# Attention products with the values: one burst for eight units, with sixteen buffers of turned probabilities

## The reference

```python
# group A: 8 heads of 64, each query sees a clamped 8 x 16 window of a 32 x 64 grid, plus a learned bias
logits = einsum('bnmqhd,bnmkhd->bnmhqk', qb, kb) * scale + bias     # masked
p = softmax(logits);  o = einsum('bnmhqk,bnmkhd->bnmqhd', p, vb)
# group B: 8 query heads on 2 key heads, |q - k| <= 128, with a sink logit per head
m = maximum(max(logits), sink)
p = exp(logits - m);  denom = sum(p) + exp(sink - m)
o = einsum('bnkgqj,bnjkd->bnqkgd', p / denom, vb)
```

## Time and profile before

| | |
|---|---|
| median of 3 runs | 2333.44 us (2331.61 to 2334.02) |
| the profiled execution | 2332.78 us, its span 2331.0 us |
| PE busy | 2223.8 us, 95% of the span |
| DVE, ACT, POOL busy | 1445.7, 922.2, 331.8 us |
| values products L890 | 1632 matmuls, 118.9 us busy, inside the attention phase |
| mean granted TensorE clock | 0.984 |

### The profile page before, as it was taken

The page is one execution under the profiler, slowest core; times in us unless marked ns, Lnnn a source line. Parts: engine busy times, 40 slices in busy tenths (PEclk is TensorE's granted clock), DMA queues, the critical chain, the costliest instruction groups (busy, mean ns, idle before and its releaser), DMA issues.

```text
span 2331.0 us, 33582 instructions
## 1 busy us (share of the span) xinstructions
PE 2223.8 (95%) x11592; PEld 1832.8 (79%) x11592; DVE 1445.7 (62%) x2761; ACT 922.2 (40%) x1790; POOL 331.8 (14%) x308
## 2 busy tenths in 40 slices
PE   7999999699979989979999999999999999999998
PEld 5888888677857868857888888788888878788886
DVE  5411023289898857768666666856565667666676
ACT  4311122178858833325333333533333333232333
POOL 6301300244390000001111212000000001010100
PEclk9999999899999999989999999999999999999999
DMA  8534333599952145666454546532323276353544
GB/s 244 160 136 136 94 98 103 147 246 245 233 149 82 55 147 202 213 233 222 172 185 167 187 165 228 200 127 77 135 78 127 69 289 234 118 173 111 176 150 153
DMA packets 278071, 376.78 MB, mean 162 GB/s; under 512 B 15578, under 2 KB 184546, under 8 KB 273328
## 3 DMA queue, kind: packets, MB, share of 16 engines
q1 hardware_dynamic: 269920, 354.21, 47.7%
q0 software_dynamic: 5568, 11.87, 2.1%
q10 hardware_dynamic: 2448, 8.91, 1.3%
HBM read 237.84 MB, written 140.31 MB: 162 GB/s over the span
## 4 chain that ended last, share of the span: by engine, by line
PE 51%; DVE 2%; DMA 1%; issue 0%; ACT 0%; DVEq 0%; ACTq 0%
PE ff_psum L1842 12%; PE ff_psum L1843 12%; PE ff_psum L1844 12%; PE ff_psum L1876 6%; PE ff_psum L1878 5%; PE ff_psum L1877 5%; DVE ff_a L1671 1%; DMA ff_raw<-in_w_gate 0%; DVE ff_x L1769 0%; DVE ff_d L1665 0%; DMA ff_d<-down_scratch 0%; DVE ff_ring L1652 0%; DVE ff_h L1657 0%; DVE ff_x L1782 0%; ACT ff_d L1541 0%
## 5 line engine op out<-in xcount | busy, mean ns | idle before, releaser
L1842 PE MATMUL ff_psum<-ff_h,ff_ring 128*128 128x512 f32 x1232 | 480.9, 390 | 14.8 <-DVE ff_ring L1652 12.5
L1843 PE MATMUL ff_psum<-ff_h,ff_ring 128*128 128x512 f32 x1232 | 480.5, 390 | 0.0
L1844 PE MATMUL ff_psum<-ff_h,ff_ring 128*128 128x512 f32 x1232 | 480.3, 390 | 0.0
L1842 PEld LDWEIGHTS ff_psum<-ff_h,ff_ring 128*128 128x128 f32 x1232 | 231.9, 188 | 63.9 <-DVEq L1718 12.9
L1843 PEld LDWEIGHTS ff_psum<-ff_h,ff_ring 128*128 128x128 f32 x1232 | 232.1, 188 | 48.2
L1844 PEld LDWEIGHTS ff_psum<-ff_h,ff_ring 128*128 128x128 f32 x1232 | 231.9, 188 | 48.3
L1876 PE MATMUL ff_psum<-ff_d,ff_a 128*128 128x512 f32 x616 | 240.6, 391 | 8.2 <-DVE ff_x L1769 5.4
L1877 PE MATMUL ff_psum<-ff_d,ff_a 128*128 128x512 f32 x616 | 239.8, 389 | 0.0
L1878 PE MATMUL ff_psum<-ff_d,ff_a 128*128 128x512 f32 x616 | 239.7, 389 | 0.0
L1769 DVE TENSOR_TENSOR ff_x<-ff_psum,ff_x 128x512 f32<-128x512 f32 x224 | 153.8, 690 | 123.3 <-PE ff_psum L1878 123.0
L1652 DVE TENSOR_TENSOR ff_ring<-ff_raw,ff_ring 128x512 fp32r<-128x512 f32 x176 | 129.7, 739 | 106.0 <-ACT ff_ring L1532 106.0
(11 more groups left out here) (149 smaller groups left out, 4136.6 us busy)
## 6 DMA issues: line engine op xcount, KB each, us to landing
acts_scratch<-ff_acts SPq DMA_DIRECT2D x22, 1792.0 KB, 7.4
ff_a<-acts_scratch SPq DMA_DIRECT2D x24, 960.0 KB, 5.0
ff_raw<-in_w_gate SPq DMA_DIRECT2D x42, 512.0 KB, 3.8
ff_raw<-in_w_up SPq DMA_DIRECT2D x42, 512.0 KB, 4.0
att_q_stack<-qk_scratch SPq DMA_DIRECT2D x64, 256.0 KB, 5.2
ff_d<-down_scratch SPq DMA_DIRECT2D x21, 768.0 KB, 6.5
ffn_in_scratch<-mix_h_stage SPq DMA_DIRECT2D x8, 1792.0 KB, 6.2
ff_h<-ffn_in_scratch SPq DMA_DIRECT2D x14, 1024.0 KB, 8.4
```

What stands on the lines that cost most here:

```text
L1842: pe.matmul(out_bank, whi[:, k], hhi[:, :, k], start=(k == 0 and not onto), stop=False, skip_group_check=onto)
L1843: pe.matmul(out_bank, whi[:, k], hlo[:, :, k], start=False, stop=False, skip_group_check=onto)
L1844: last = pe.matmul(out_bank, wlo[:, k], hhi[:, :, k], start=False, stop=(k == 3), skip_group_check=onto)
```

## The change

`values` does nothing in seven of eight units; in the last of a block (u % 8 = 7) it waits once and then issues the products of all four tiles, 24 or 32 (22 where a tile has two chunks) times a chunk's pair of heads. The buffers of turned probabilities grow from 4 to 16. `pv_done` counts blocks instead of tiles, and the waits on it are rewritten to match. Lags, order of stages and every other buffer stay.

```diff
-    SC_BUFS, SN_BUFS, PT_BANKS, PT_BUFS, O_BANKS = 4, 8, 2, 4, 2
+    SC_BUFS, SN_BUFS, PT_BANKS, PT_BUFS, O_BANKS = 4, 8, 2, 16, 2
+    GROUP = 8
@@ advance (SyncE)
-                        sp.wait_ge(pv_done, PT_BUFS // 2 + NT * r + 4 * (b + 1))
+                        sp.wait_ge(pv_done, 2 + 4 * r + b + 1)
@@ copy_turned (ACT)
-                act.wait_ge(pv_done, PT_BUFS // 2 + NT * r + u // 2 - 1)
+                act.wait_ge(pv_done, 4 * r + u // GROUP + 1)
@@ results (DVE)
-                dve.wait_ge(pv_done, PT_BUFS // 2 + NT * r + 4 * (b + 1))
+                dve.wait_ge(pv_done, 2 + 4 * r + b + 1)
@@ values (PE)
-                if u % 2 == 0:
+                if u % GROUP != GROUP - 1:
                     return
-                t = u // 2
-                b, n = t // 4, kind.chunks(t)
-                for i in kind.new_portions(t):
-                    pe.wait_ge(v_in[i], 16 * (r + 1) if kind.near else 16 * (NEAR_ROUNDS + 1))
+                b = u // GROUP
+                for t in range(4 * b, 4 * b + 4):
+                    for i in kind.new_portions(t):
+                        pe.wait_ge(v_in[i], 16 * (r + 1) if kind.near else 16 * (NEAR_ROUNDS + 1))
                 pe.wait_ge(pt_copied, PT_BANKS + UNITS * r + u + 1)
-                if t % 4 == 0:
-                    pe.wait_ge(o_copied, 4 * r + b + 1)
-                for j in range(n):
-                    v = v_sb[:, kind.value_chunk(t, j), :]
-                    for e in range(2):
-                        h = slice(e * HD, (e + 1) * HD)
-                        last = pe.matmul(op[h, b % 2, t % 4 * P:(t % 4 + 1) * P], v[:, h],
-                                         pt[:, (u - 1 + e) % PT_BUFS, j * P:(j + 1) * P],
-                                         start=(j == 0), stop=(j == n - 1))
+                pe.wait_ge(o_copied, 4 * r + b + 1)
+                for t in range(4 * b, 4 * b + 4):
+                    n = kind.chunks(t)
+                    for j in range(n):
+                        v = v_sb[:, kind.value_chunk(t, j), :]
+                        for e in range(2):
+                            h = slice(e * HD, (e + 1) * HD)
+                            last = pe.matmul(op[h, b % 2, t % 4 * P:(t % 4 + 1) * P], v[:, h],
+                                             pt[:, (2 * t + e) % PT_BUFS, j * P:(j + 1) * P],
+                                             start=(j == 0), stop=(j == n - 1))
                 last.then_inc(pv_done, 1)
-            pe.sem_inc(pv_done, PT_BUFS // 2)
+            pe.sem_inc(pv_done, 2)
```

## The result

The changed kernel takes 2361.11 us (median of 4, 2355.85 to 2363.20), the kernel before 2333.73 (median of 4): a ratio of 1.0115, 95% interval 1.0096 to 1.0133, so it is slower by 27 us. The forecast was 2354, and slower. The profiled execution took 2355.85 us, with a span of 2354.0: against the profiled one of before, 2332.78, that is 23.1 us where the sum gave 21.5.

What follows compares the result with a forecast made beforehand. The prediction took PE to bound the attention phase, with DVE and ACT close behind. Loops lengthened by uncovered bursts summed to 21.5 us more, added to the profiled 2332.8: 2354 us, range 2340 to 2364.

Steps and rivals of the forecast that it cites:

- 0.34 us for each visit to the products: PE's passage between tile forms around a visit to the products; 96 fewer visits take 33 us off PE's time.
- The burst is not covered: Attention phase: ACT stands still during PE's burst; its copies and exps make a 10.3 us loop against 9.5 on average before.
- Window rounds 41.1: Sum of four block loops in a window round, 10.1, 10.3, 10.8 and 9.9 us: 3.2 us more than before.
- Near rounds 45.2: Sum of four block loops in a near round, 11.6, 11.9, 11.0 and 10.7 us: 1.8 us more than before.
- 1.5 for GpSimd: Near rounds: GpSimd's bias making slows DVE's normalise, now on the loop's path; 1.5 us a round, between 0 and some 5.
- The other terms: Remaining shares of the sum by round, such as 1 us for round 0 and 2.5 each for rounds 3 and 4.
- PE's idle time: Expected sign: in window rounds it rises from 3% to some 20%, ahead of the turn and released by ACT's copy.
- DMAs don't move: SyncE's waits on `pv_done` stay for a block's last tile, some 2 us later; next round's values are needed a round later.
- the third rival: Nothing measurable: loss in window rounds and gain in near ones cancel, within 5 us of 2333; chance 0.06.
- PE as the bound: Rival: PE stays the bound in the attention phase, so the 33 us of passages come out, 2300 us; chance 0.06.
- DVE as the bound: Rival: the burst is hidden and DVE's own work bounds the rounds, 2320 us if half is met; chance 0.12.

Runs made afterwards that it cites:

- one_form: Kernel before with one full-width product per chunk instead of two half-width ones, head 1's share left out: 2313.67 us, 0.9919 of the kernel before.
- first_chunk: Changed kernel with only the first chunk's product of each tile, in the same bursts: 2320.75 us, 0.9940 of the kernel before.
- late_results: Changed kernel with DVE copying a block's results out in step u + 12 instead of u + 8: 2349.85 us, 1.0073 of the kernel before.
- few_bias: Changed kernel with GpSimd making one of six bias operations of each kind in near rounds 1 to 3: 2355.48 us, 1.0090 of the kernel before.
- group4: Changed kernel with the products of two tiles in one burst instead of four: 2331.59 us, 0.9985 of the kernel before.
- group4_late: Changed kernel with bursts of two tiles and the results' copy in step u + 12: 2343.32 us, 1.0042 of the kernel before.

## Why the prediction was right

- *PE bound the attention phase, with 0.34 us for each visit to the products.* Right but for one block in four of a window round: one_form shows the size (0.32 to 0.33) and the cause, and its cycle with the sinks stays at 10.57, DVE's, as in the kernel before.
- *The burst is not covered, and the loop from burst to burst goes through ACT's copies and exps.* Right and shown: first_chunk takes the burst's length out of the loop one for one, late_results takes out DVE's copy. The link from the last exp to the last copy and the turn is read in the trace, no run took it out alone; the timeline above has the turn 0.15 behind the copy's end.
- *Window rounds 41.1.* Measured 41.5. By block 10.1, 10.3, 10.8 and 9.9 were given; from the turn ahead of a burst to the next such turn it is 10.13, 10.34, 11.01 and 10.02 (turns at 771.34, 781.47, 791.81, 802.82 and 812.84).
- *Near rounds 45.2 and 1.5 for GpSimd.* 45.55 (few_bias) and 1.9. By block 11.6, 11.9, 11.0 and 10.7 were given for the bare loops; from turn to turn few_bias has 11.64, 11.95, 11.17 and 10.79 in round 1, and the changed kernel 12.38, 12.41, 11.86 and 10.79 in round 2.
- *The other terms.* From the places of the results' copies: round 0 +1.3 (1 given), rounds 1 and 2 +7.6 (6.6), rounds 3 and 4 together +3.0 (5.0), 5 and 6 +7.2 (6.4), round 7 with the tail +3.5 (2.5): 22.7, and the rest of the program is unchanged to half a microsecond. That the sum is only 1.2 off is in part luck: the terms of rounds 3 and 4 were 2.0 too large and the others together 3.2 too small. For the mechanism the loops by block are the better evidence.
- *The executions without a profile* lie some 5 us above the profiled one in the changed kernel, both times, and not in the one before. Of the 7 us by which the median is above the forecast they are 5.3, and the terms 1.6. No trace shows where these 5 us are. They need not be in the attention phase: from the last results' copy to the end the profiled executions take 1510.1 us before and 1510.4 in the changed kernel, but 1511.8 when it was run again and 1515.1 in first_chunk, though no edit touches that part.
- *PE's idle time of "some 20%" in window rounds* was too much: it is 13% by windows. The 20% came from distances from start to start (1.9 of 10.3 in the working), whereas busy times reach to an instruction's modelled end and cover short gaps.
- *"DMAs don't move"* held for the change. It would not have for a later results' copy: I took SyncE's order as harmless without asking what stands behind the store.
- *Slips in the working.* DVE's own work in a window round adds up to 34.9 us, not 34.8. DVE at 90% in near rounds leaves a tenth of PE's work, not an eighth. For the third rival near rounds 0 to 3 would have had to be some 4.5 us a round shorter ((21.5 - 4.7) / 3.75), not 2.5. None of them enters the sum.

Of the rivals, PE as the bound and DVE as the bound both gave a faster kernel. What they lack is the same: PE's and ACT's lists are in program order, so a piece of work put in one place delays everything listed behind it, and the other engine's list stops at its first entry that needs it.

## What to carry to other kernels

Grouping work on the busiest engine saves its passages only as long as the engines behind it have queued work for the whole burst; lay out one loop from burst to burst with the latencies between engines, and compare it with the busy sum. Here 96 passages of 0.34 us were worth 33 us, and four tiles in a burst turned that into a loss of 27; 64 passages, 22 us, became a gain of 3.5 with two tiles. When a saving falls short, look for the block in which another engine was the bound before the change: the cycle with the sinks, 10.57 before, is 10.56 or 10.57 in first_chunk, one_form and group4 alike.

## What the runs showed that I had not expected

- One product of the full width takes PE about as long as the two half-width ones of two heads: 0.59 us for three chunks (six matmuls, 552.33 to 552.92) against 0.64 (twelve matmuls, six pairs of 0.107). So the two heads' halves of the array do work side by side.
- A copy of 0.6 us moved by four steps on DVE cost 12 us (group4 to group4_late) through a third party, SyncE's queue of loads, and moving a store behind those loads won them back.
